# Dense v phase of a PEER layer: the gates of four experts per load in runs of 1 KB, in place of pairs in runs of 512 bytes

## The chip, the cores and the metric

One core of one Trainium2 chip runs the whole layer as one program. The metric is device time in microseconds, the median over runs. Everything is float32; most matmuls take operands that are split into a high and a low part (float32r), three matmuls for one product.

## What is computed

One layer of a streaming encoder over 1024 tokens of width 1024: gated mixing and attention, cross attention to a memory, then a PEER channel layer with 16384 single-neuron experts. Only the last part matters here:

```python
g = softmax(gv)                    # 128 picked experts per token
u = expert_u[idx_blk]
a = g_blk * gelu(einsum('tkd,td->tk', u, x_blk))
out = einsum('tk,tkd->td', a, expert_v[idx_blk])
h = layer_norm(DN_ALPHA * h + out)
```

## The kernel before

**Two ways for the experts.** The first 512 tokens (4 tiles, `GT`) fetch their picked rows of `expert_u` and `expert_v` by indirect DMAs that GpSimd issues (L1488), 128 rows of 4 KB each, into a ring of 8 slots (`ex_ring`). VectorE turns a u row tile into one dot per token (L1497); TensorE adds four v row tiles at a time into `ex_ps_v` (L1513, "values": 16 matmuls). The last 512 tokens (`DT` = 4 tiles) are computed densely over all 16384 experts, as 128 tiles of 128 experts. The dense u phase stores the activations of each expert tile to `act_d` in HBM (256 KB each). A gate phase then builds the gates of the 512 tokens and stores them to `gate_d`, whose shape is [8 token blocks, 128 partitions, 128 expert tiles, 64 tokens], so the 64 tokens of one expert tile are a run of 256 bytes and neighbouring expert tiles lie behind one another.

**The dense v phase** (from L1999 on) is the stage that the change touches. It multiplies activation by gate and adds a·v over the 128 expert tiles, in 32 groups of `GE` = 4. The gathers, dots and values of the first 512 tokens go on beside it. Its loop per expert tile e is:

- SyncE (queue q1, hardware_dynamic) loads a (`act_d`, 256 KB, L2045) once the low part of a of expert e-2 is done, and v (`expert_v`, 512 KB, L2050) once the low part of v of expert e-2 is done. The first four experts go through other buffers (L2038, L2039).
- SyncE loads gates for two expert tiles at a time with one DMA (`load_gates`, L2035): 128 partitions x 8 blocks, runs of 2 x 256 = 512 bytes, 512 KB. There are two buffers. After v of an even expert e it loads the pair e+2, e+3, once the product of expert e-1 is made, since that frees the buffer.
- ScalarE copies v to its high part (L2079), VectorE makes a times gate in place (`multiply`, L2108), ScalarE copies that to the high part of a (L2081), VectorE makes the low parts of v and a (L2113, L2115).
- VectorE then adds one finished PSUM tile of the group before to `eo_acc` (L2123; in the first group L2121), and does one dot of the gather tokens (L1497), the latter up to expert tile 67.

TensorE does a group when the low parts of its four experts are there: four token tiles, each of 24 matmuls of 128x512 (L110 to L112), with `values` between them. It writes two PSUM buffers in turn, so its tile t waits for VectorE's add of tile t-2. High and low parts have two group buffers. So VectorE works on group q+1 while TensorE works on group q, and each engine's order is written out by hand:

```python
for x in range(GE):
    multiply(q * GE + x)
    low_parts(q * GE + x)
    if q >= 1:
        add(q - 1, x)
    for _ in range(dots_b(q * GE + x)):
        dot(dve, done)
```

SyncE's queue is in order: a wait of one load holds back every load behind it. GpSimd's gathers run on queue q0 (software_dynamic), over the same 16 DMA engines.

Of the kernel before, what the change touches and what calls it, by code (L numbers as in the profile page):

```python
# [23 lines left out]
ALU = mybir.AluOpType  # L24
AX = mybir.AxisListType

P = 128
D = 1024
# [24 lines left out]
GBLK = 64  # L53
# [6 lines left out]
def layer_program(nc, x, mem, ln_in_g, ln_in_b, w_in, gate_ln_g, gate_ln_b, w_sp, b_sp, rel_bias, w_out,  # L60
# [4 lines left out]
    def dram(name, shape):  # L65
        return nc.dram_tensor(name, shape, F32, kind="Internal").ap()
# [15 lines left out]
    gate_d = dram("gate_d", [T // 2 // GBLK, P, P, GBLK])  # L82
# [3 lines left out]
    def sem(name):  # L86
        stage_sems.append(nc.alloc_semaphore(name=name))
        return stage_sems[-1]
# [7 lines left out]
    def local(stage):  # L96
        def sb(name, shape, dt=F32):
            return stage.enter_context(nc.sbuf_tensor(name, shape, dt))

        def pb(name, cols):  # L100
            return stage.enter_context(nc.psum_tensor(name, [P, cols], F32))
        return sb, pb
# [11 lines left out]
    with top:  # L114
# [16 lines left out]
        with ExitStack() as stage:  # L131
            sb, pb = local(stage)
# [1189 lines left out]
        def expert_stages(gain, bias, resid, dest):  # L1322
# [4 lines left out]
            DN = DT * P  # L1327
            ETILES = P
            RING, EXTRA, EXTRA_G = 8, 7, 5
            GE = 4  # L1330
            GROUPS = ETILES // GE
            NBLK = DN // GBLK
# [108 lines left out]
            gate_stored = [sem(f"ex_gate_stored{i}") for i in range(2)]  # L1441
            a_in = [sem(f"eo_a_in{i}") for i in range(2)]
            v_in = [sem(f"eo_v_in{i}") for i in range(2)]
            g_in = [sem(f"eo_g_in{i}") for i in range(2)]
            prod, a_hi_done, a_lo_done = sem("eo_prod"), sem("eo_a_hi"), sem("eo_a_lo")
            v_hi_done, v_lo_done = sem("eo_v_hi"), sem("eo_v_lo")
            out_mm = [sem(f"eo_mm{i}") for i in range(2)]
# [5 lines left out]
            with ExitStack() as whole:  # L1453
# [95 lines left out]
                with ExitStack() as gating:  # L1549
# [4 lines left out]
                    with ExitStack() as stage:  # L1554
                        sb, pb = local(stage)
# [328 lines left out]
                    with ExitStack() as stage:  # L1884
                        sb, pb = local(stage)
# [117 lines left out]
                with ExitStack() as stage:  # L2003
                    sb, pb = local(stage)
                    ln = RowNorm("eo_ln", sb, gain, bias, rows=(ring[:, 0, :], ring[:, 1, :]))
                    acc = sb("eo_acc", [P, DT, D])
                    a_sb, v_sb, g_raw = sb("eo_a_raw", [P, 2, DN]), sb("eo_v_raw", [P, 2, D]), sb("eo_g_raw", [P, 2, NBLK, 2, GBLK])
                    a_hi, a_lo = [w[:].rearrange("p (b x) t -> p b x t", b=2) for w in (late_hi, late_lo)]
                    v_hi, v_lo = sb("eo_v_hi_sb", [P, 2, GE, D], F32R), sb("eo_v_lo_sb", [P, 2, GE, D], F32R)
                    ps = [pb(f"eo_ps{i}", D) for i in range(2)]  # L2010
# [1 line left out]
                    def a_raw(e):  # L2012
                        return v_sb[:, e // 2, e % 2 * DN:(e % 2 + 1) * DN] if e < GE else a_sb[:, e % 2, :]

                    def v_raw(e):
                        return acc[:, e, :] if e < GE else v_sb[:, e % 2, :]

                    def loaded(eng, sems, e):
                        if e < GE:
                            eng.wait_ge(first_in[e], 32)  # L2020
                        else:
                            eng.wait_ge(sems[e % 2], 16 * ((e - GE) // 2 + 1))

                    def whole_row(j):
                        return xg[:, j, :] if j < GT else acc[:, j - GT, :]
# [3 lines left out]
                    with nc.Block() as block:  # L2029
                        @block.sync  # L2030
                        def _(sp):
                            def load_gates(r):
                                if r >= 2:
                                    sp.wait_ge(prod, 2 * (r - 1))
                                sp.dma_start(g_raw[:, r % 2, :, :, :], gate_d[:, :, 2 * r:2 * r + 2, :].rearrange("n p e t -> p n e t")).then_inc(g_in[r % 2], 16)  # L2035

                            for e in range(GE):
                                sp.dma_start(v_raw(e), v_rows[e, :, :]).then_inc(first_in[e], 16)  # L2038
                                sp.dma_start(a_raw(e), act_d[e, :, :]).then_inc(first_in[e], 16)  # L2039
                                if e % 2 == 0:  # L2040
                                    load_gates(e // 2)
                            for e in range(GE, ETILES):
                                if e >= GE + 2:
                                    sp.wait_ge(a_lo_done, e - 1)
                                sp.dma_start(a_raw(e), act_d[e, :, :]).then_inc(a_in[e % 2], 16)  # L2045
                                if e >= GE + 2:
                                    sp.wait_ge(v_lo_done, e - 1)
                                else:
                                    sp.wait_ge(a_lo_done, 2 * (e - GE + 1))
                                sp.dma_start(v_raw(e), v_rows[e, :, :]).then_inc(v_in[e % 2], 16)  # L2050
                                if e == GE:
                                    load_gates(GE // 2)
                                if e % 2 == 0 and e // 2 + 1 < ETILES // 2:
                                    load_gates(e // 2 + 1)
                                if e < 2 * GE:
                                    t = e - GE
                                    sp.wait_ge(v_lo_done, t + 1)
                                    sp.dma_start(acc[:, t, :], resid[(GT + t) * P:(GT + t + 1) * P, :]).then_inc(row_in[t], 16)
                                if e == LN_TILES * GE:
                                    sp.wait_ge(val_done, GT * P // 4)  # L2060
                                    ln.load(sp)
                            for j in range(TT):
                                sp.wait_ge(ln.ln_done, j + 1)
                                sp.dma_start(dest[j * P:(j + 1) * P, :], whole_row(j)).then_inc(stored, 16)
                            sp.wait_ge(stored, 16 * TT)
# [34 lines left out]
                        @block.vector  # L2100
                        def _(dve):
                            def multiply(e):
                                r = e // 2
                                loaded(dve, a_in, e)
                                if e % 2 == 0:
                                    dve.wait_ge(g_in[r % 2], 16 * (r // 2 + 1))
                                a = a_raw(e).rearrange("p (n t) -> p n t", t=GBLK)
                                dve.tensor_tensor(a, a, g_raw[:, r % 2, :, e % 2, :], ALU.mult).then_inc(prod, 1)  # L2108

                            def low_parts(e):  # L2110
                                b, x = e // GE % 2, e % GE
# [95 lines left out]
        free_sems()  # L2207
        early_stack.close()
        expert_stages(ln3_g, ln3_b, h2_d, out)
        act_stack.close()  # L2210

# [26 lines left out]
```

## Time and profile before

| What | Value |
|---|---|
| Median of 3 runs | 3495.75 us (3494.16 to 3499.4) |
| The profiled execution's own time | 3511.59 us |
| Its span | 3509.7 us |
| Mean granted TensorE clock | 0.94 |
| Dense v phase in it | first load 2582.7 us, first matmul 2611.3 us, last add about 3491 us |

The page divides the span into 40 slices of 87.7 us; the dense v phase is the last eleven. TensorE's row of the page is 9 (over 90% busy) in nearly all of them, and so is the DMA row until the last two. The time of the phase is therefore read from three things: how much TensorE idles in it, what VectorE, which feeds it, waits for, and what a load takes from its issue to its landing.

### The profile page before, as it was taken

Reading aid. Unit: us, or ns where it says so; the run is one execution under the profiler, and the core shown is the slowest. Engines: PE = TensorE matmul, PEld = TensorE weight load, DVE = VectorE, ACT = ScalarE, POOL = GpSimd, SP = SyncE. Lnnn points to the kernel's source line nnn. Section 1 sums busy time; section 2 is a strip of 40 time slices with the busy share of each in tenths; the row PEclk is TensorE's granted clock in tenths of the full one; section 3 lists DMA queues with packets and bytes.
Section 4 is the critical chain, followed back from the end, with each engine's and each line's share of the span. In section 5 each row is a group of like instructions: output and inputs, shape, how many; then the busy total and the mean of one; then the engine's idle time right before and its main releaser. Section 6 shows DMA issues by size and latency. Waiting matters only on the chain. (4 is left out here: it accounts for less than half of the span.)

```text
span 3509.7 us, 42739 instructions
## 1 busy us (share of the span) xinstructions
PE 3071.8 (88%) x16184; PEld 2393.6 (68%) x16184; DVE 2150.3 (61%) x4547; ACT 1137.3 (32%) x1739; POOL 1480.2 (42%) x1116
## 2 busy tenths in 40 slices
PE   3996888788879979999999999977749999999996
PEld 3875676677768867787777777655527676676665
DVE  4144684313545758987888776587737667654456
ACT  3212452312321114333333333287712222222222
POOL 3100102420120026885877677687734444434432
PEclk9997599899989989999999999988969999999998
DMA  4333003322222259999999999999999999989992
GB/s 159 102 108 119 20 2 126 125 88 65 107 102 63 71 207 351 412 408 374 408 410 402 410 410 383 374 365 406 410 348 344 357 378 383 373 304 372 374 350 100
DMA packets 367516, 936.06 MB, mean 267 GB/s; under 512 B 32832, under 2 KB 129736, under 8 KB 366288
## 3 DMA queue, kind: packets, MB, share of 16 engines
q0 software_dynamic: 147456, 536.94, 39.2%
q1 hardware_dynamic: 219856, 396.39, 31.4%
q8 instruction: 130, 2.13, 0.2%
q14 instruction: 74, 0.61, 0.0%
HBM read 825.53 MB, written 107.67 MB: 266 GB/s over the span
## 5 line engine op out<-in xcount | busy, mean ns | idle before, releaser
L1488 POOL DMA_INDIRECT ex_ring<-in_expert_v,ex_idxT_sb x405 | 475.8, 1175 | 513.8 <-PE ex_ps_v L1513 225.2
L1488 POOL DMA_INDIRECT ex_ring<-in_expert_u,ex_idx_sb x307 | 392.3, 1278 | 201.5 <-issue 87.8
L110 PE MATMUL eo_ps<-eo_v_hi_sb,aT_late_hi 128*128 128x512 f32 x1024 | 410.9, 401 | 41.5 <-DVE aT_late_lo L2115 41.5
L110 PE MATMUL ex_ps_h<-aT_late_hi,ex_uT_hi_sb 128*128 128x512 f32 x1024 | 415.4, 406 | 24.9 <-ACT ex_act L1656 12.4
L1497 DVE CUSTOM_DVE_ANT_0 ex_ring<-ex_ring,ex_xg 128x1024 f32<-128x1024 f32 x307 | 368.4, 1220 | 92.6 <-DMA ex_ring<-in_expert_u,ex_idx_sb 64.9
L112 PE MATMUL ex_ps_h<-aT_late_hi,ex_uT_lo_sb 128*128 128x512 f32 x1024 | 403.9, 394 | 0.0
L111 PE MATMUL eo_ps<-eo_v_lo_sb,aT_late_hi 128*128 128x512 f32 x1024 | 403.5, 394 | 0.0
L111 PE MATMUL ex_ps_h<-aT_late_lo,ex_uT_hi_sb 128*128 128x512 f32 x1024 | 402.7, 393 | 0.0
L112 PE MATMUL eo_ps<-eo_v_hi_sb,aT_late_lo 128*128 128x512 f32 x1024 | 402.3, 393 | 0.0
L2123 DVE TENSOR_TENSOR eo_acc<-eo_acc,eo_ps 128x1024 f32<-128x1024 f32 x124 | 151.4, 1221 | 280.8 <-PE eo_ps L112 215.2
L1513 PE MATMUL ex_ps_v<-ex_ring,ex_w_sb 128*32 128x512 f32 x1620 | 233.1, 629 | 75.6 <-DMA ex_ring<-in_expert_v,ex_idxT_sb 62.5
L1497 DVE CUSTOM_DVE_ANT_0 ex_ring_more<-ex_ring_more,ex_xg 128x1024 f32<-128x1024 f32 x193 | 230.5, 1220 | 100.9 <-DMA ex_ring_more<-in_expert_u,ex_idx_sb 74.6
L110 PEld LDWEIGHTS eo_ps<-eo_v_hi_sb,aT_late_hi 128*128 128x128 f32 x1024 | 194.6, 190 | 136.7 <-issue 52.8
L1488 POOL DMA_INDIRECT ex_ring_more<-in_expert_u,ex_idx_sb x193 | 246.1, 1275 | 70.6 <-issue 57.9
L110 PEld LDWEIGHTS ex_ps_h<-aT_late_hi,ex_uT_hi_sb 128*128 128x128 f32 x1024 | 194.4, 190 | 99.4 <-issue 51.3
L2079 ACT ACTIVATE eo_v_hi_sb<-eo_v_raw 128x1024 fp32r<-128x1024 f32 x124 | 131.3, 1059 | 395.6 <-DMA eo_v_raw<-in_expert_v 305.2
L1644 ACT ACTIVATE ex_uT_lo_sb<-ex_ps_t 128x1024 fp32r<-128x1024 f32 x128 | 131.7, 1029 | 373.6 <-PE ex_ps_t L1830 263.6
L112 PEld LDWEIGHTS ex_ps_h<-aT_late_hi,ex_uT_lo_sb 128*128 128x128 f32 x1024 | 194.7, 190 | 43.1
L112 PEld LDWEIGHTS eo_ps<-eo_v_hi_sb,aT_late_lo 128*128 128x128 f32 x1024 | 194.4, 190 | 42.3
L111 PEld LDWEIGHTS eo_ps<-eo_v_lo_sb,aT_late_hi 128*128 128x128 f32 x1024 | 194.6, 190 | 38.5
L111 PEld LDWEIGHTS ex_ps_h<-aT_late_lo,ex_uT_hi_sb 128*128 128x128 f32 x1024 | 195.0, 190 | 37.1
L2113 DVE TENSOR_TENSOR eo_v_lo_sb<-eo_v_raw,eo_v_hi_sb 128x1024 fp32r<-128x1024 f32 x124 | 157.9, 1274 | 32.6 <-ACT eo_v_hi_sb L2079 28.2
(351 smaller groups left out, 6445.4 us busy)
## 6 DMA issues: line engine op xcount, KB each, us to landing
ex_u_raw<-in_expert_u SPq DMA_DIRECT2D x128, 512.0 KB
eo_v_raw<-in_expert_v SPq DMA_DIRECT2D x124, 512.0 KB
act_d<-ex_act SPq DMA_DIRECT2D x128, 256.0 KB
gate_d<-ex_gate SPq DMA_DIRECT2D x8, 4096.0 KB, 15.1
eo_g_raw<-gate_d SPq DMA_DIRECT2D x64, 512.0 KB
eo_a_raw<-act_d SPq DMA_DIRECT2D x124, 256.0 KB
h_d<-n_row SPq DMA_DIRECT2D x24, 512.0 KB, 2.6
pin_raw<-in_w_in SPq DMA_DIRECT2D x20, 512.0 KB
```

Of the source, the lines that this page charges most:

```text
L110: pe.matmul(ps, l_hi, r_hi, start=first, stop=False)
L111: pe.matmul(ps, l_hi, r_lo, start=False, stop=False)
L112: return pe.matmul(ps, l_lo, r_hi, start=False, stop=last)
L1488: pool.indirect_dma_start(rows(n), None, table, bass.IndirectOffsetOnAxis(at, 0)).then_inc(ring_in[slot[n]], 16)
L1497: dve.tensor_tensor_reduce(out=u, in0=u, in1=xg[:, j, :], scale=1.0, scalar=0.0, op0=ALU.mult, op1=ALU.add, accum_out=hg[:, j, k:k + 1]).t ...
L1513: last = pe.matmul(ps_v[32 * q:32 * q + 32, col], spreads[:, q, 31 * i + 31:31 * i + 63], rows(at[q])[:, col], start=i == 0, stop=i == 31)
L1644: act.activation(uT_lo[:, e % 2, :, :], ps_t[e % 2][:].rearrange("p (k t) -> p k t", t=P), ACT.Copy).then_inc(uT_lo_done, 1)
L2079: act.activation(v_hi[:, b, x, :], v_raw(e), ACT.Copy).then_inc(v_hi_done, 1)
L2113: dve.tensor_tensor(v_lo[:, b, x, :], v_raw(e), v_hi[:, b, x, :], ALU.subtract).then_inc(v_lo_done, 1)
L2123: dve.tensor_tensor(acc[:, t, :], acc[:, t, :], ps[t % 2][:], ALU.add).then_inc(added[t % 2], 1)
```

## The change

Gates are loaded for a group of four expert tiles into one buffer of the same total size as the two before, [128, 8 blocks, 4 experts, 64 tokens]. The runs are 4 x 256 bytes = 1 KB. Each load is two DMAs of four blocks (512 KB each) on one semaphore, and the first product of the group waits for both (32). `load_gates(q)` comes after v of expert 4q, as a load did before, and with the same wait, that the product of expert 4q-1 is made. But what it loads is the gates of experts 4q to 4q+3, where it was those of 4q+2 and 4q+3. The load after v of expert 4q+2 is gone.

```diff
-            g_in = [sem(f"eo_g_in{i}") for i in range(2)]
+            g_in = sem("eo_g_in")
...
-g_raw = sb("eo_g_raw", [P, 2, NBLK, 2, GBLK])
+g_raw = sb("eo_g_raw", [P, NBLK, GE, GBLK])
...
-                            def load_gates(r):
-                                if r >= 2:
-                                    sp.wait_ge(prod, 2 * (r - 1))
-                                sp.dma_start(g_raw[:, r % 2, :, :, :], gate_d[:, :, 2 * r:2 * r + 2, :].rearrange("n p e t -> p n e t")).then_inc(g_in[r % 2], 16)
+                            def load_gates(q):
+                                if q >= 1:
+                                    sp.wait_ge(prod, GE * q)
+                                for h in range(2):
+                                    n = slice(h * NBLK // 2, (h + 1) * NBLK // 2)
+                                    sp.dma_start(g_raw[:, n, :, :], gate_d[n, :, GE * q:GE * (q + 1), :].rearrange("n p e t -> p n e t")).then_inc(g_in, 16)
...
-                                if e % 2 == 0:
-                                    load_gates(e // 2)
+                                if e == 0:
+                                    load_gates(0)
...
-                                if e == GE:
-                                    load_gates(GE // 2)
-                                if e % 2 == 0 and e // 2 + 1 < ETILES // 2:
-                                    load_gates(e // 2 + 1)
+                                if e % GE == 0:
+                                    load_gates(e // GE)
...
-                                r = e // 2
                                 loaded(dve, a_in, e)
-                                if e % 2 == 0:
-                                    dve.wait_ge(g_in[r % 2], 16 * (r // 2 + 1))
+                                if e % GE == 0:
+                                    dve.wait_ge(g_in, 32 * (e // GE + 1))
                                 a = a_raw(e).rearrange("p (n t) -> p n t", t=GBLK)
-                                dve.tensor_tensor(a, a, g_raw[:, r % 2, :, e % 2, :], ALU.mult).then_inc(prod, 1)
+                                dve.tensor_tensor(a, a, g_raw[:, :, e % GE, :], ALU.mult).then_inc(prod, 1)
```

## Rows read from the trace of the kernel before

**Rows 1.** Busy time by stage of the dense v phase (windows of the span).

```profile
core 0: us, PE busy (x) PEld busy (x) DVE busy (x) ACT busy (x) POOL busy (x), PEclk, DMA share, GB/s
2583.00:2611.00 28.00, 0.28 (x1) 0.00 (x0) 12.90 (x18) 7.42 (x9) 9.13 (x10) 0.50 1.01 363
2611.00:2700.00 89.00, 85.28 (x382) 63.99 (x383) 64.99 (x84) 22.81 (x28) 29.52 (x27) 0.94 0.93 339
2700.00:3100.00 400.00, 383.78 (x1870) 278.18 (x1870) 266.61 (x335) 98.27 (x119) 176.29 (x162) 1.00 1.00 368
3100.00:3400.00 300.00, 295.43 (x1503) 202.33 (x1502) 151.99 (x170) 70.75 (x86) 131.66 (x123) 1.00 0.98 359
3400.00:3491.00 91.00, 79.67 (x345) 62.00 (x344) 66.09 (x90) 25.10 (x33) 15.05 (x7) 0.94 0.41 144
```

**Rows 2.** Who waited for whom, 2700 to 3100 us: total, times, longest.

```profile
DVE eo_acc L2123 <- PE eo_ps L112: 82.2, 45, 4.6
DVE eo_acc L2123 <- issue: 25.2, 8, 4.8
PE ex_ps_v L1513 <- DMA ex_ring<-in_expert_v,ex_idxT_sb: 13.2, 13, 1.9
PE eo_ps L110 <- DVE aT_late_lo L2115: 3.1, 2, 2.6
```

**Rows 3.** Chain that ended last, pieces of 2738 to 3008 us: start, length, what.

```profile
2741.04 14.09 DMA eo_a_raw<-act_d
...
2857.01 1.22 DVE ex_ring L1497
...
2861.70 7.59 DMA ex_ring<-in_expert_v,ex_idxT_sb
...
2869.42 1.92 PE ex_ps_v L1513 x16
...
2882.16 9.32 DMA eo_v_raw<-in_expert_v
...
2894.81 8.37 DMA eo_v_raw<-in_expert_v
...
2906.15 12.49 DMA eo_a_raw<-act_d
...
2923.20 10.07 DMA eo_v_raw<-in_expert_v
...
2990.02 8.59 DMA eo_v_raw<-in_expert_v
```

**Rows 4.** DMA queues in 3432.4 to 3435.2 us: packets, MB, share of 16 engines.

```profile
DMA packets 1040, 0.52 MB, mean 187 GB/s; under 512 B 16, under 2 KB 1040, under 8 KB 1040
q1 hardware_dynamic: 1040, 0.52, 63.6%
```

**Rows 5.** DMA queues in 1532.3 to 1534.0 us (gathers beside one load of 1-KB runs).

```profile
q0 software_dynamic: 150, 0.55, 81.8%
q1 hardware_dynamic: 148, 0.13, 22.7%
```

**Rows 6.** DMA queues and gate issues in 2700 to 3100 us.

```profile
DMA packets 71535, 147.32 MB, mean 368 GB/s; under 512 B 4968, under 2 KB 35688, under 8 KB 71514
q0 software_dynamic: 23218, 84.54, 55.4%
eo_g_raw<-gate_d SPq DMA_DIRECT2D x29, 512.0 KB
```

**Rows 7.** VectorE in order of time, from expert 39's product to expert 43's.

```profile
2852.72 0.69 DVE L2108 TENSOR_TENSOR eo_a_raw<-eo_a_raw,eo_g_raw 128x512 f32<-128x512 f32 x1
...
2858.16 0.69 DVE L2108 TENSOR_TENSOR eo_a_raw<-eo_a_raw,eo_g_raw 128x512 f32<-128x512 f32 x1
...
2863.66 1.22 DVE L2123 TENSOR_TENSOR eo_acc<-eo_acc,eo_ps 128x1024 f32<-128x1024 f32 x1 [3.07 <-issue]
...
2865.94 0.69 DVE L2108 TENSOR_TENSOR eo_a_raw<-eo_a_raw,eo_g_raw 128x512 f32<-128x512 f32 x1
...
2869.09 1.22 DVE L2123 TENSOR_TENSOR eo_acc<-eo_acc,eo_ps 128x1024 f32<-128x1024 f32 x1 [0.69 <-PE eo_ps L112]
...
2877.06 1.22 DVE L2123 TENSOR_TENSOR eo_acc<-eo_acc,eo_ps 128x1024 f32<-128x1024 f32 x1 [3.24 <-PE eo_ps L112]
```

**Rows 8.** SyncE's queue: one gate load in the loaded stretch, one near the end.

```profile
2853.43 0.37 SPq L2035 DMA_DIRECT2D eo_g_raw<-gate_d  x1
...
3431.48 0.37 SPq L2035 DMA_DIRECT2D eo_g_raw<-gate_d  x1
```

**Rows 9.** VectorE in order of time at a later group boundary, without dots.

```profile
3226.51 0.69 DVE L2108 TENSOR_TENSOR eo_a_raw<-eo_a_raw,eo_g_raw 128x512 f32<-128x512 f32 x1
...
3233.97 1.22 DVE L2123 TENSOR_TENSOR eo_acc<-eo_acc,eo_ps 128x1024 f32<-128x1024 f32 x1 [5.04 <-issue]
3235.11 0.68 DVE L2108 TENSOR_TENSOR eo_a_raw<-eo_a_raw,eo_g_raw 128x512 f32<-128x512 f32 x1
```

**Rows 10.** VectorE in order of time, start of the phase.

```profile
2596.51 0.69 DVE L2108 TENSOR_TENSOR eo_v_raw<-eo_v_raw,eo_g_raw 128x512 f32<-128x512 f32 x1 [12.31 <-DMA eo_g_raw<-gate_d]
...
2600.86 0.69 DVE L2108 TENSOR_TENSOR eo_v_raw<-eo_v_raw,eo_g_raw 128x512 f32<-128x512 f32 x1 [1.93 <-DMA eo_v_raw<-act_d]
...
2605.38 0.69 DVE L2108 TENSOR_TENSOR eo_v_raw<-eo_v_raw,eo_g_raw 128x512 f32<-128x512 f32 x1 [0.46 <-DMA eo_g_raw<-gate_d]
...
2608.87 0.69 DVE L2108 TENSOR_TENSOR eo_v_raw<-eo_v_raw,eo_g_raw 128x512 f32<-128x512 f32 x1
...
2612.36 0.69 DVE L2108 TENSOR_TENSOR eo_a_raw<-eo_a_raw,eo_g_raw 128x512 f32<-128x512 f32 x1
...
2619.96 1.22 DVE L2121 SCALAR_TENSOR_TENSOR eo_acc<-eo_acc,eo_ps 128x1024 f32<-128x1024 f32 x1 [5.17 <-PE eo_ps L112]
```

**Rows 11.** The products by tile: count, durations and what they waited for.

```profile
L2108 DVE TENSOR_TENSOR eo_a_raw<-eo_a_raw,eo_g_raw x124: 680/686/721, 2612.4 to 3460.9; 128x512 f32<-128x512 f32 x124
L2035 SPq DMA_DIRECT2D eo_g_raw<-gate_d x64: 370/371/743, 2583.5 to 3431.5; - x64
  DMA eo_g_raw<-gate_d: 12.8, 2
```

**Rows 12.** The page's 40 slices of 87.7 us: GB/s that the DMA engines moved.

```profile
GB/s 159 102 108 119 20 2 126 125 88 65 107 102 63 71 207 351 412 408 374 408 410 402 410 410 383 374 365 406 410 348 344 357 378 383 373 304 372 374 350 100
```

More of the change, by code:

```diff
@@ L2006, in expert_stages @@
                     acc = sb("eo_acc", [P, DT, D])
-                    a_sb, v_sb, g_raw = sb("eo_a_raw", [P, 2, DN]), sb("eo_v_raw", [P, 2, D]), sb("eo_g_raw", [P, 2, NBLK, 2, GBLK])
+                    a_sb, v_sb, g_raw = sb("eo_a_raw", [P, 2, DN]), sb("eo_v_raw", [P, 2, D]), sb("eo_g_raw", [P, NBLK, GE, GBLK])
                     a_hi, a_lo = [w[:].rearrange("p (b x) t -> p b x t", b=2) for w in (late_hi, late_lo)]
```

## The prediction

> **What bounds the kernel now.** I read the busy time by stage first [rows 1]. From 2700 to 3400 us TensorE is busy 679 of 700 us, and the DMA share is 1.00 and 0.98. So this stage has two limits side by side: TensorE has 16.2 us of idle time in the first 400 us and 4.6 us in the next 300, and the DMA engines hardly rest. Then who waited for whom [rows 2]: VectorE's adds wait 107.4 us in 400 for TensorE's tiles, whereas TensorE waits only 3.1 us for low parts and 13.2 us for gathered v rows. VectorE, the one reader of the gates, therefore has slack: 29 gate loads of two experts in 400 us [rows 6] are 14.5 groups, one per 27.6 us, and 107.4 / 14.5 = 7.4 us of each group is waiting before adds. The chain that ended last [rows 3] passes through TensorE, and where it leaves it, it goes through transfers: gathers that a dot releases (7.6 us), v loads (8.4 to 10.1 us), and twice an a load that stands behind a gate load (14.1 and 12.5 us). The gates themselves stop a product only twice in the whole phase, 12.8 us together, both in the start [rows 10, 11].
>
> Two things can therefore move the time: a little less DMA work, and a gate load that now has to arrive within one step of VectorE, where it had three.
>
> **The sum, part by part.** It is made against the profiled execution of 3511.59 us (span 3509.7), and the difference is then put on the median of 3495.75, which is 15.8 us lower.
>
> 1. *Instructions.* 64 gate issues of 0.37 us become 32 x 2. SyncE's queue carries as many as before, GpSimd's queue isn't touched, the products read the same number of elements (686 ns) [rows 11]. At expert 4q the wait stands where it stood, with the same count; at 4q+2 it goes, but the next thing in the queue waits for a later event anyway (low part of a of 4q+1). Cost 0. The cover is that SyncE does nothing else.
>
> 2. *Packets.* A 512-byte packet costs 0.636 x 2.8 us x 16 / 1024 = 27.8 ns [rows 4] (1024 packets and 16 completion marks). A 1-KB packet costs 0.227 x 1.7 us x 16 / 128 = 48.2 ns [rows 5] (a 128-KB load of score rows, beside gathers). A 4-KB one costs 0.554 x 400 us x 16 / 20640 = 172 ns [rows 6] (84.54 MB are 20640 of them), 43 ns per KB. So 1 KB of gates goes from 55.6 to 48.2 ns, with bounds of 55.6 (no gain) and 43. There are 64 x 512 = 32768 KB: 15.2 us of 16 engines over the phase (0 to 25.8), 0.47 us per group. I take 48.2, as it is the same kind of load. How much arrives at the end? From 2611 to 3100 us (17.7 groups, 8.3 us saved) the chain goes through transfers part of the time; I give it half, -4 us, since TensorE's idle time there can give back no more than some 20 us in all (16.2 + 3.7). After 3100 TensorE is 98% busy [rows 1]: 0. Bounds: 0 and -16.
>
>    The Trainium skill (DMA: Bandwidth & Descriptors, Specifications) says that 512 bytes is the smallest transfer for line rate. By that rule the longer runs would bring nothing and this term would be 0; the rows at 27.8 and 48.2 ns speak against it, by 13% of the gates' share. The same page (Why small descriptors are slow) has a fixed cost of about 3 cycles per packet beside one per 32 bytes, so 38 cycles become 35, 8%; by that estimate the term would be -2.5 us.
>
> 3. *The exposed load.* Before, a load issued at the end of the product of 4q-1 was for experts 4q+2 on. Now it is for 4q, the very next product. In rows 7 the product of expert 39 ends at 2853.41, the gate load is issued at 2853.43 [rows 8], and the next product starts at 2858.16: 4.75 us. Without dots it is 7.9 us (3227.2 to 3235.1) [rows 9]. What does the load take? Idle, 1024 packets take 1.0 us to start and 2.6 us to move (issue at 3431.48, packets inside 3432.4 to 3435.2 [rows 4, 8]); 1024 packets of 1 KB 48.2 - 27.8 = 20.4 ns x 64 per engine = 1.3 us more, 5 us. Loaded, four v loads of the same queue take 9.1 us on average [rows 3]; they stand behind a gate load issued shortly before, so a gate load lands 1 to 2 us earlier than that, and the longer packets give 1.3 us back: 9 us. The bounds are 5 us and 14.1 us. So the first product of a group comes 9 - 4.75 = 4.2 us late while dots run.
>
>    Who is behind it on VectorE: low parts, the add of tile 0, a dot (which frees a gather slot), then the next expert. The waits before these adds are 3.07, 0.69 and 3.24 us [rows 7], so 4.2 us late becomes 1.2 at the first dot, 0.5 at the second, 0 at the third. TensorE needs the add of tile 0 only before tile 2, a whole tile (about 6.9 us) later, and the low parts only at the group's end: covered. What isn't covered is the gather behind a late dot, where it is on the chain. I take a quarter of a us per group of the 17 groups with dots: +4 us. Bounds: 0 (all covered), and the rival below. After expert 67 the boundary gap is 7.9 us, and the wait before the next add up to 5 us: 0. In the last two groups the DMA engines are nearly idle (0.41), the load takes 5 us: 0.
>
> 4. *What stands behind the gates on SyncE's queue.* a and v of expert 4q+1 now follow 1 MB, 1.3 us later than before, but their product starts later by more. a and v of 4q+3 have nothing before them any more and come up to 1.8 us earlier (1024 x 27.8 / 16). On the chain both kinds occur (the 14.1 and the 12.5 us are such a loads). 0, with -3 to +5.
>
> 5. *The start.* The first product waits 12.31 us for gates [rows 10]; that load is twice as large in as many packets, +1.3 us. The third product's 0.46 us wait for gates goes. First matmul +0.8 us, bounds -2 and +3. The gates of expert 4 are now issued after the product of expert 3 (2609.6) and land 6 to 7 us later, 4 us after the 2612.36 of before; the add behind them waits 5.17 us for TensorE [rows 10], so that is covered.
>
> Sum: 0 - 4 + 4 + 0 + 0.8 = +0.8 us, 3512.4 for the profiled execution, **3497 us** for the median, rounded up by half a us, as the bounds reach further up. About 0.2% (7 us) is what a measurement of this kernel can tell from no change.
>
> **The rivals.**
>
> *A. The DMA engines are the real limit of the dot stretch* (faster). For it: share 1.00 at 2700 to 3100, TensorE idle 16.2 us there, v loads and gathers on the chain. Then the whole saving of the stretch arrives, 8.3 us, and with shorter queues in front of gathers and of a and v of expert 4q+3 another 3: 3495.75 - 11 + 0.8 = 3485 us. Against it: TensorE's own work is 96% of the stretch, and 147.32 MB in 400 us is 368 GB/s, while the same engines moved 402 to 412 in most slices of the phase before [rows 12].
>
> *B. The single buffer closes a loop* (slower). Product of 4q-1, gate load, product of 4q, three more experts, next load. VectorE's step without waits is 7.78 - 3.07 = 4.71 us [rows 7], so the loop is 3 x 4.7 + 0.7 + L = 14.8 + L us. It decides above L = 27.6 - 14.8 = 12.8 us. Two of the transfers of rows 3 are above or near that, five are well below. If every load of groups 1 to 17 took 14.1 us, the period would be 28.9: +1.3 x 17 = 22 us, 3518. With half of them so, and late gathers besides, 3508.
>
> *C. The change doesn't do what it says* (slower): a 1-KB packet costs twice a 512-byte one beside the gathers, or the doubled burst delays the gathers released just then (the dot at 2857.0 and its gather at 2861.7 fall beside the load of 2853.43). Then term 2 is 0 and term 3 about doubles: +9, 3505 us.
>
> **How the numbers follow.** Forecast (all hidden or paid back, 3489 to 3502): 0.40. A 0.29, B 0.21, C 0.10. The range has to leave out 2 in 10: A's own bound is 3480, B's full price 3518, so 3480 to 3517. Faster by over 0.2% is A, 0.29; within it 0.40; slower B and C, 0.31. The likeliest case alone has 3489 to 3502.
>
> **What the profile of the changed kernel would show.** Queue q1 loses 32768 packets of 512 bytes at equal MB; if its share times the span doesn't fall by some 15 us, term 2 is wrong. The products of experts 4q wait for gates: some 3 us a time in the first 17 groups, 30 to 60 us in all, near none after expert 72. VectorE's waits for TensorE's tiles shrink by about as much. TensorE's idle time from 2700 to 3100 stays within some 8 us of 16.2. The first matmul comes at about 2612 us. I would be wrong if TensorE waits for low parts by tens of us (B), or if waits for gathers fall well below 13 us and the stretch shortens (A), or if the waits before products of experts 4q average over 6 us.

## The result and the profile after

**3543.3 us** median of 4 runs (3541.5 to 3556.9) against 3495.0 (4 runs) for the kernel before: ratio 1.0144, 95% interval 1.0117 to 1.0171, 48 us slower. The forecast was 3497, the range ended at 3517. The profiled execution took 3556.91 us (span 3555.0), 45.3 more than that of before. The dense v phase begins 6.0 us earlier in it, so the phase itself is some 51 us longer.

The windows of the dense v phase after the change, cut as in [rows 1] (its first load is at 2576.6 us, before at 2582.7):

```profile
core 0: us, PE busy (x) PEld busy (x) DVE busy (x) ACT busy (x) POOL busy (x), PEclk, DMA share, GB/s
2583.00:2611.00 28.00, 4.50 (x11) 3.58 (x12) 12.91 (x18) 6.53 (x8) 5.76 (x6) 0.50 0.94 345
2611.00:2700.00 89.00, 83.38 (x395) 63.21 (x394) 61.92 (x80) 21.91 (x27) 27.67 (x25) 1.00 0.89 327
2700.00:3100.00 400.00, 351.63 (x1647) 246.92 (x1645) 242.17 (x307) 87.66 (x105) 170.04 (x149) 0.94 0.91 332
3100.00:3400.00 300.00, 293.26 (x1477) 203.34 (x1474) 154.49 (x174) 71.92 (x88) 123.65 (x115) 0.99 0.94 350
3400.00:3536.00 136.00, 124.33 (x577) 91.70 (x576) 87.71 (x115) 35.37 (x45) 38.11 (x28) 0.96 0.62 221
```

The loss is in 2700 to 3100, where dots and gathers run: TensorE is idle 48.4 us there in place of 16.2, and does 1647 matmuls in place of 1870; the DMA share falls from 1.00 to 0.91. No engine is busier than before; they wait in turn. Who waited for whom, 2700 to 3100 (total, times, longest), against [rows 2]:

```profile
DVE eo_a_raw L2107 <- DMA eo_g_raw<-gate_d: 90.5, 13, 11.4
...
DVE eo_acc L2122 <- PE eo_ps L112: 58.1, 16, 8.7
...
PE ex_ps_v L1513 <- DMA ex_ring<-in_expert_v,ex_idxT_sb: 43.2, 13, 6.6
```

Each of the 13 groups stops VectorE at its first product for 7 us. VectorE's waits before its adds shrink from 107.4 us (82.2 for TensorE's tiles, 25.2 for nothing that the profile names) to 58.1, as the slack is eaten. And TensorE waits 43.2 us for gathered v rows, where it waited 13.2: that is 30 of the 32 us of new idle time. The groups of TensorE's lines in the same window, before the change and after it (busy, mean ns of one, idle before), say where the rest is:

```profile
L1513 PE MATMUL ex_ps_v<-ex_ring,ex_w_sb 128*32 128x512 f32 x448 | 53.9, 597 | 13.2 <-DMA ex_ring<-in_expert_v,ex_idxT_sb 13.2
```

```profile
L110 PE MATMUL eo_ps<-eo_v_hi_sb,aT_late_hi 128*128 128x512 f32 x416 | 166.9, 401 | 5.1 <-DVE eo_acc L2122 3.5 <-DVE aT_late_lo L2114 1.6
L111 PE MATMUL eo_ps<-eo_v_lo_sb,aT_late_hi 128*128 128x512 f32 x415 | 163.0, 393 | 0.0
L112 PE MATMUL eo_ps<-eo_v_hi_sb,aT_late_lo 128*128 128x512 f32 x416 | 162.7, 391 | 0.0
L1513 PE MATMUL ex_ps_v<-ex_ring,ex_w_sb 128*32 128x512 f32 x400 | 60.5, 731 | 43.3 <-DMA ex_ring<-in_expert_v,ex_idxT_sb 43.2
```

The dense matmuls run at their old speed. The values matmuls, which come right behind the wait, take 60.5 us for 400, where before's rate (53.9 / 448) gives 48.1: 12.4 us more. Windows of 5 us around one such wait show why:

```profile
2910.00:2915.00 5.00, 5.00 (x23) 4.13 (x22) 5.00 (x7) 1.70 (x2) 3.35 (x3) 1.00 0.73 257
2915.00:2920.00 5.00, 0.42 (x2) 0.00 (x0) 5.00 (x9) 0.63 (x1) 4.08 (x4) 0.81 0.93 304
2920.00:2925.00 5.00, 2.98 (x16) 0.67 (x16) 2.43 (x3) 1.58 (x2) 1.74 (x2) 0.51 1.00 395
2925.00:2930.00 5.00, 5.00 (x25) 3.90 (x22) 0.00 (x0) 0.00 (x0) 3.43 (x4) 1.00 1.04 389
```

TensorE stands still from 2915.4 to 2922.0, the granted clock falls to 0.51 (the lower level, 1.2 of 2.4 GHz), and most of the 16 values matmuls run at it. The chain has both cases: 16 values matmuls right behind a wait, and the next 16 with none before them.

```profile
2808.62 3.64 PE ex_ps_v L1513 x16
...
2823.39 1.85 PE ex_ps_v L1513 x16
```

Of the 25 sets of 16 in this window the eight behind the longest waits take 3.0 to 3.6 us and the other 17 some 1.9 each, and this difference is the whole 12.4 us. So a wait costs its own length and then slow matmuls: 30.0 + 12.4 us, and some 2 us before adds and low parts: 44 us in this window.

The chain that ended last shows the loop itself (start, length, what):

```profile
2859.99 0.37 SPq L2037
2860.40 15.66 DMA eo_g_raw<-gate_d
2876.15 0.69 DVE eo_a_raw L2107
2876.85 1.13 DVE eo_v_lo_sb L2112
2877.98 0.60 DVE aT_late_lo L2114
2878.58 1.13 DVE eo_acc L2122
2879.71 1.14 DVE ex_ring L1497
2880.86 0.60 DVE eo_a_raw L2107
...
2890.78 0.37 SPq L2037
2891.20 14.77 DMA eo_g_raw<-gate_d
2906.06 0.69 DVE eo_a_raw L2107
...
2921.05 17.42 DMA eo_g_raw<-gate_d
```

The load takes 15.66 us, then VectorE works with no wait from 2876.15 to 2890.77, from the product of expert 4q to that of 4q+3, then comes the next load: 30.8 and 29.9 us a round. The other gate loads on this chain are 16.86, 16.66 and 16.87 us. From TensorE's first matmul of group 1 to that of group 17 it is 30.2 us per group on average (27.2 before): 16 x 2.94 = 47 us. From group 17 to 31 it is 28.5 us (28.2 before), 4 us more over 14 of them.

### The profile page after: what moved, and what is told of

Its sections match the earlier page's. It is cut to its first block and busy times, and to the rows that moved or that the text cites. A ratio compares the mean times of both kernels' runs of the same rounds, so it can differ in the third digit from the quotient of the medians.

```text
span 3555.0 us, 42707 instructions
## 1 busy us (share of the span) xinstructions
PE 3086.1 (87%) x16184; PEld 2397.9 (67%) x16184; DVE 2150.1 (60%) x4547; ACT 1137.9 (32%) x1739; POOL 1487.2 (42%) x1116
## 3 DMA queue, kind: packets, MB, share of 16 engines
q1 hardware_dynamic: 187088, 396.39, 30.8%
## 5 line engine op out<-in xcount | busy, mean ns | idle before, releaser
L1488 POOL DMA_INDIRECT ex_ring<-in_expert_v,ex_idxT_sb x405 | 465.7, 1150 | 544.5 <-PE ex_ps_v L1513 253.3
L1513 PE MATMUL ex_ps_v<-ex_ring,ex_w_sb 128*32 128x512 f32 x1620 | 244.1, 658 | 114.6 <-DMA ex_ring<-in_expert_v,ex_idxT_sb 99.5
L1488 POOL DMA_INDIRECT ex_ring_more<-in_expert_u,ex_idx_sb x193 | 261.9, 1357 | 77.7 <-issue 57.0
L1513 PEld LDWEIGHTS ex_ps_v<-ex_ring,ex_w_sb 128*32 128x32 f32 x1620 | 52.3, 115 | 215.0 <-issue 213.5
```

What stands on the lines that cost most here:

```text
L1488: pool.indirect_dma_start(rows(n), None, table, bass.IndirectOffsetOnAxis(at, 0)).then_inc(ring_in[slot[n]], 16)
L1513: last = pe.matmul(ps_v[32 * q:32 * q + 32, col], spreads[:, q, 31 * i + 31:31 * i + 63], rows(at[q])[:, col], start=i == 0, stop=i == 31)
```

## The experiments

Ratios are to runs of the kernel before on the same chip, with 95% intervals. "Before" and "after" are the two kernels of this study.

**Is it the runs or the place of the load?** e1 keeps before's two buffers, counts and places and has the pair buffer filled in 1-KB runs (four experts, half of the blocks), so that some products take gates of another expert or block. e2 keeps 512-byte runs and loads both pairs where the changed kernel loads the four. e3 is the changed kernel with runs of 4 KB (16 experts of one block), again with other experts' gates.

```diff
 e1, against before
-  sp.dma_start(g_raw[:, r % 2, :, :, :], gate_d[:, :, 2 * r:2 * r + 2, :]...
+  half, quad = slice(r % 2 * NBLK // 2, (r % 2 + 1) * NBLK // 2), slice(r // 2 * GE, r // 2 * GE + GE)
+  sp.dma_start(g_raw[:, r % 2, :, :, :]..., gate_d[half, :, quad, :]...
 e2, against before
-      sp.wait_ge(prod, 2 * (r - 1))
+      sp.wait_ge(prod, r // 2 * GE)
-  if e % 2 == 0 and e // 2 + 1 < ETILES // 2:
+  if e % GE == 0:
+      load_gates(e // 2)
       load_gates(e // 2 + 1)
 e3, against after
-  n = slice(h * NBLK // 2, (h + 1) * NBLK // 2)
+  n, e0 = ..., 32 * (q % 4) + 16 * h
+  sp.dma_start(g_raw[:, n, :, :]..., gate_d[q // 4, :, e0:e0 + 16, :])
```

> The kernel before, its two pair buffers, places and waits untouched; only each 512-KB gate load reads 512 runs of 1 KB in place of 1024 runs of 512 bytes (it fetches half the blocks of a group of four experts, so products take gates of other experts and blocks). Theory (the late issue costs, not the runs): 16-engine time of gates falls by 15 us, the median is 3480 to 3495 us. Rival R (1-KB runs at this pitch are themselves dear or crowd the gathers): 3505 us or more.

> The kernel before with 512-byte runs and two pair buffers, but both pairs of a group are loaded where the changed kernel loads its four experts (after v of expert 4q, once the product of 4q-1 is made), and the first product of the group waits for both. Theory (late issue, and each packet may wait one turn behind a gather packet): 2048 packets in place of 1024, so the load takes longer than the 16.5 us of the changed kernel, 17 to 25 us, and the median is 3550 to 3640 us. Rival B (only the bytes of the burst count): as the changed kernel, 3543 within 7 us. Rival R (the runs are to blame): about 3500 us.

> The changed kernel with its timing and 2 x 512 KB per group, but each load reads 128 runs of 4 KB (gates of other experts), 256 packets per group in place of 1024. Theory (turns per packet): 16 packets per engine meet at most 16 gather packets of 172 ns, so the load takes 4 us of queue + about 6 us = 9 to 11 us, the loop 14.8 + 10 = 25 us is under TensorE's 27.6, and the median is 3490 to 3507 us. Rival B (bytes shared evenly between queues): the load still takes 14 to 17 us and the median stays within 10 us of 3543.

e1: 0.9983 (0.9950 to 1.0016). e2: 1.0217 (1.0147 to 1.0288). e3: 1.0025 (0.9994 to 1.0057). The times of e1, e2 and e3 came out as the first theory of each had it. Loading a whole group's gates late and together makes the loss, with 512-byte runs too; the 1-KB runs in the old places cost at most 0.2%. Whether the longer runs soften the loss isn't shown, since the intervals of e2 and of the changed kernel overlap. In e2 the same two waits of 2700 to 3100 are larger still:

```profile
DVE eo_a_raw L2109 <- DMA eo_g_raw<-gate_d: 107.3, 13, 16.0
...
PE ex_ps_v L1513 <- DMA ex_ring<-in_expert_v,ex_idxT_sb: 50.8, 13, 6.7
```

with gate loads of up to 20.2 us on its chain. In e3, with a fourth of the packets for the same bytes, two gate loads are on the chain of that window, and they are far shorter:

```profile
2870.88 10.66 DMA eo_g_raw<-gate_d
...
2955.57 10.57 DMA eo_g_raw<-gate_d
```

From the issue of a gate load to the start of the product that needs it, it is 9.4 us on average in this window (6.6 to 12.7), against 15.8 after the change. 14.6 + 10.6 = 25.2 us is under the 27.2 of a group before: a late load costs little (0.6% at most, perhaps nothing) if it is short enough.

**What makes the load long?** e9 loads pairs of 512-byte runs, each only when the product before it is made: twice as many exposed loads as after, each of as many packets (1024) but half the bytes. e10 and e11 are after and before with the ring's gathers cut to a quarter of each row (1 KB), so dots and values take the rest from what the slot held.

```diff
 e9, against before
-      sp.wait_ge(prod, 2 * (r - 1))
+      sp.wait_ge(prod, 2 * r)
-  if e % 2 == 0 and e // 2 + 1 < ETILES // 2:
-      load_gates(e // 2 + 1)
+  if e % 2 == 0:
+      load_gates(e // 2)
 e10, e11, against after and before
+  w = D if n < END_G else D // 4
-  pool.indirect_dma_start(rows(n), None, table, ...
+  pool.indirect_dma_start(rows(n)[:, 0:w], None, table.rearrange("r (a c) -> (r a) c", c=w), ...
```

> The kernel before with 512-byte runs and pairs, but each pair is loaded only once the product just before the pair is made (one product ahead in place of three), so 512 KB are exposed twice per group. Theory: a load of 1024 packets takes 11 to 16 us beside the gathers as in the changed kernel, whatever its bytes, so a pair's loop is 4.7 + 0.7 + L = 16 to 21 us, 33 to 42 us per group in the dot stretch: 60 to 150 us slower than before, worse than the changed kernel. Rival (bytes count): half the bytes land in half the time, 8 us, the loop is 2 x 13.5 = 27 us, and it is within 15 us of before.

> The changed kernel; in the dense v phase each gather fetches 1 KB per row in place of 4 KB (other bytes, so dots and values of that phase are of other data). All instructions and waits stay. Theory (the gate load is long because gather packets stand between its own): the load takes 6 to 9 us instead of 16, the loop of 15 + 8 = 23 us is under TensorE's time, and the kernel is within 8 us of the next control. Rival (the load's length is its own, from its packets and their pitch in HBM): it takes 13 us or more and the distance to the control stays 35 us or more.

> Control: the kernel before with the same short gathers. Both theories: 5 to 25 us faster than before, since values and dots no longer wait for gathers.

e9: 1.0127 (1.0103 to 1.0151), 40 us. Both expectations missed the time (60 us or more, 15 at most); on the length of a load the rival, that bytes count, was right with its 8 us. The waits are many (197.5 us at 50 products) but the loads short. The chain has seven of 7.9 to 8.3 us in a row, three of them:

```profile
2795.69 7.93 DMA eo_g_raw<-gate_d
2807.91 8.04 DMA eo_g_raw<-gate_d
2821.38 7.90 DMA eo_g_raw<-gate_d
```

e10: 0.9909 (0.9893 to 0.9926), e11: 0.9904 (0.9886 to 0.9922). With short gathers, the changed kernel and the kernel before differ by 3 us (3461.8 and 3458.6), as the theory had it. Against the kernel before with whole gathers e11 is 36 us faster, more than the 5 to 25 that were expected. The windows 2700 to 3100 of e10 and of e11:

```profile
2700.00:3100.00 400.00, 400.00 (x1954) 291.67 (x1952) 275.82 (x343) 102.16 (x125) 175.23 (x162) 1.00 0.65 217
```

```profile
2700.00:3100.00 400.00, 400.00 (x1960) 290.38 (x1959) 277.50 (x345) 104.58 (x127) 175.08 (x160) 1.00 0.67 217
```

TensorE never rests in either. The place and the bytes of the load are the same as after, so the gathers beside it make its length. The table is from the packets in the traces: for the gate loads issued between 2690 and 3080 us, the mean time from issue to last packet, and what the gather queue moved between first and last packet (e8, e12 and e15 are described below):

| kernel | load, packets of | us | gathers beside it, MB | their GB/s |
|---|---|---|---|---|
| before | 1024 of 512 B | 8.2 | 1.10 | 185 |
| e1, early, longer runs | 512 of 1 KB | 6.7 | 0.69 | 149 |
| e9, late pairs | 1024 of 512 B | 7.6 | 0.81 | 156 |
| after | 1024 of 1 KB | 15.1 | 2.74 | 244 |
| e2, late pairs together | 2048 of 512 B | 16.7 | 3.04 | 239 |
| e12, one group ahead | 1024 of 1 KB | 10.4 | 1.50 | 170 |
| e15, as e12 | 1024 of 1 KB | 10.3 | 1.39 | 169 |
| e8, after, 6 ring slots | 1024 of 1 KB | 8.1 | 0.85 | 125 |
| e10, after, short gathers | 1024 of 1 KB | 5.2 | 0.10 | 25 |

A load that lasts longer meets more gathers by that alone, so the megabytes don't prove the cause; e10 does, and the last column, a rate, doesn't have this fault. Two things make the 15 us together. The load has twice the bytes: half of them in the late place take 7.6 us (e9), no longer than before. And it stands in a dense stretch of gathers: the same bytes one group ahead take 10.4 us (e12).

Why the gathers are dense just there is argued from the order of the rows, no run tests it by itself. While VectorE waits it frees no slot, and then dots come 4.65 us apart (rows 2879.71, 2884.37 and 2889.01 of the chain, and a fourth behind the next load's issue), each with a new 512-KB gather, and values free four more slots; the next gate load is issued right behind them. At its issue 1.01 MB of gathers are issued and not yet moved, against 0.84 before and 0.38 in e12. If that is the reason, the loop feeds itself.

**Does it help to take the dots out of the loop?** e4 makes all dots of a group before its first product.

```diff
+  for _ in range(sum(dots_b(q * GE + x) for x in range(GE))):
+      dot(dve, done)
+      done += 1
   for x in range(GE):
...
-      for _ in range(dots_b(q * GE + x)):
-          dot(dve, done)
-          done += 1
```

> The changed kernel with VectorE's order changed: all dots of a group come before its first product, so they run while the gates are under way. Theory (a loop of product, load, three more experts, load bounds the dot stretch; late dots make gathers late): three dots of 1.2 us leave the loop, 14.8 + 16.5 = 31.3 becomes 27.7 us, and no dot waits for gates: 3500 to 3515 us. Rival (TensorE loses to the DMA burst itself, that is to gathers slowed by it): 3535 us or more.

e4: 1.0241 (1.0184 to 1.0298), a miss for the theory; the rival's time came true, but by another path. The gate loads did get short (8.6 us beside 0.70 MB), but other waits of 2700 to 3100 took their place:

```profile
DVE ex_ring L1497 <- DMA ex_ring<-in_expert_u,ex_idx_sb: 99.8, 17, 11.6
...
PE eo_ps L110 <- DVE eo_acc L2122: 53.7, 12, 8.7
```

Four dots in a row outrun their gathers, VectorE waits for those, and its adds come too late for TensorE.

**A second buffer of four.** There is no room for one beside the ring. e6 takes ring slots 6 and 7; e7 and e8 are before and after with a ring of 6, as controls.

```diff
 e6, e7, e8
-  slot.append((n - END_G) % RING)
+  slot.append((n - END_G) % (RING - 2))
 e6 besides, against after
+  g_raw = [sb("eo_g_raw", ...), ring[:, 6:8, :]...]
-  if q >= 1:
-      sp.wait_ge(prod, GE * q)
+  if q >= 2:
+      sp.wait_ge(prod, GE * (q - 1))
+  if e % GE == 0 and e // GE + 1 < GROUPS:
+      load_gates(e // GE + 1)
```

> The changed kernel's loads (2 x 512 KB of 1-KB runs per group) with a second buffer, so that each group's gates are loaded one group ahead, once the last product of the group before last is made. The buffer lies in two slots of the gather ring, which has 6 slots in the dense v phase; so it is to be read against the kernel before with 6 slots. Theory (exposure alone costs): it equals that control or is up to 12 us faster, and no product waits for gates after the first. Rival (the burst of 1 MB hurts gathers, a and v by itself): 15 us or more above that control.

> Control: the kernel before with 6 ring slots in the dense v phase. Both theories: 0 to 30 us slower than before, since two gathers fewer are under way.

> Control: the changed kernel with 6 ring slots in the dense v phase. Theory: at most 6 gathers, in place of 8, can stand beside the gate load, so the load lands 1 to 4 us sooner, and the time is 25 to 50 us above the control of the kernel before with 6 slots. Rival (gathers do not set the load's time): the load takes the same 15 to 17 us and the distance stays 48 us or more.

e6: 1.0415 (1.0376 to 1.0454), e7: 1.0437 (1.0384 to 1.0491), e8: 1.0428 (1.0374 to 1.0482). Two slots fewer cost 145 us (3653.7 against 3508.4) where 30 at most were expected, and hide everything else: all three are equal, and nothing follows for the buffer. e8 misses both of its expectations (25 us or more above e7; it is 5). Its late loads took only 8.1 us, beside gathers at half the rate of after: with fewer gathers under way, the late load is short and the change costs nothing that can be measured.

**The second buffer elsewhere.** e12 parks two tiles of `ex_xg` (1 MB, unused until the layer norm) in HBM, puts the second buffer there and loads each group of four one group ahead. e13 is the control: before, with the same tiles parked and used as ring slots 8 and 9.

```diff
 e12, against after
+  g_raw = [sb("eo_g_raw", ...), xg[:, 0:2, :]...]
+  sp.wait_ge(sum_g, 2)
+  sp.dma_start(park_d..., xg[:, 0:2, :]).then_inc(parked, 16)
-  if e % GE == 0:
-      load_gates(e // GE)
+  if e % GE == 0 and e // GE + 1 < GROUPS - 1:
+      load_gates(e // GE + 1)
   if e == LN_TILES * GE:
+      sp.dma_start(xg[:, 0:2, :], park_d...).then_inc(back, 16)
 e13, against before (parking as in e12)
-  slot.append((n - END_G) % RING)
+  slot.append((n - END_G) % (RING + 2))
```

> The changed kernel's loads (2 x 512 KB of 1-KB runs per group) with a second buffer and the full ring of 8 slots. The buffer is the place of the first two finished token tiles, which are written to HBM (1 MB) at the start of the phase and read back before their norm; gates are loaded one group ahead from group 1 to 30. Theory (the missing lead of the load is the whole loss): all of the 48 us come back, the median is 3485 to 3500 us on the scale of 3495, and no product between expert 8 and 123 waits for gates. Rival (bursts of 1 MB or 1-KB runs cost by themselves): 3515 us or more.

> The kernel before with the same two tiles parked in HBM, the place used for two more slots of the gather ring (10 in place of 8) in the dense v phase; gates as before. Since 6 slots cost 150 us, gathers have little to spare at 8. If TensorE's waits for gathers are the rest of the loss in the dot stretch, 10 slots give 5 to 20 us: 3475 to 3490 us. If more gathers under way only lengthen the a, v and gate loads, 3495 us or more.

e12: 1.0075 (1.0046 to 1.0103), 3522 us on the scale of 3495, which is the rival's side. e13: 0.9987 (0.9956 to 1.0018), 3491 us: ten slots with the parking equal eight without it, less than the theory's gain. So the lead gives about half of the 48 us back. Its products no longer wait for gates, but v loads of up to 17 us stand on its chain: SyncE issues them behind two gate loads, 1 MB in one piece. That alone proves nothing, since e13's chain has v loads of 17.4 and 18.7 us at no loss of time. e14 issues the second half two experts later; e15 is e12 again, on e14's chip.

```diff
 e14, against e12
-  if e % GE == 0 and e // GE + 1 < GROUPS - 1:
-      load_gates(e // GE + 1)
+  if e % (GE // 2) == 0 and e // GE + 1 < GROUPS - 1:
+      load_gates(e // GE + 1, (e % GE // 2,))
```

> e12 (a second buffer for four experts' gates, each load one group ahead, runs of 1 KB) with the two 512-KB halves of a load issued two experts apart, after v of expert 4q and after v of expert 4q+2, in place of one behind the other. Theory (what is left of e12's excess is the 1-MB burst ahead of SyncE's next loads of a and v): the loads of v on the chain of waits, 9.7 to 17.1 us in e12, come back to 8 to 11 us as before the change; the time is within 0.4% of the kernel before on the same chip (ratio 0.996 to 1.004). Rival (the rest lies elsewhere: the lead shares the gathers' bandwidth in a worse place whatever the size of the piece, or the first execution's chip was at fault): the ratio stays at 1.005 or above, and the chain's loads of v stay above 11 us.

> e12 once more, on the same chip as e14, since e12's one comparison was made on a chip whose runs of the kernel before lay 20 us apart. Both theories: 1.005 to 1.010 again, and by theory above e14. If it comes within 0.4% of the kernel before, e12's excess was that chip's, and the lead alone gives the whole loss back.

e14: 1.0022 (1.0008 to 1.0036). e15: 1.0052 (1.0034 to 1.0071). ScalarE's wait for v in 2700 to 3100, in e15 and then in e14:

```profile
ACT eo_v_hi_sb L2096 <- DMA eo_v_raw<-in_expert_v: 177.9, 46, 15.1
```

```profile
ACT eo_v_hi_sb L2096 <- DMA eo_v_raw<-in_expert_v: 126.0, 47, 5.9
```

The longest wait for v falls from 15.1 to 5.9 us, e15's chain has a v load of 19.05 us in this window and e14's has none, and TensorE waits 12.6 us for gathers in e14 (23.1 in e15, 13.2 before). Both came out as their theories had it, though the intervals of e14 and e15 just touch. A lead with the load in two pieces brings the time back to within 0.2% (8 us on that chip) of the kernel before; e14 parks its tiles as e12 does, so the parking costs no more than that.

**The 1-KB runs with the old places and the right gates.** e5 changes the layout in HBM, so that two blocks of 64 tokens lie side by side: a pair of experts is then in runs of 1 KB, and the gate phase stores runs of 256 bytes.

```diff
-  gate_d = dram("gate_d", [T // 2 // GBLK, P, P, GBLK])
+  gate_d = dram("gate_d", [T // 4 // GBLK, P, P, 2 * GBLK])
-  sp.dma_start(gate_d[n], gate_sb[:, n % 2, :, :])
+  sp.dma_start(gate_d[n // 2, :, :, n % 2 * GBLK:(n % 2 + 1) * GBLK], gate_sb[:, n % 2, :, :])
```

> The kernel before, all its waits and places kept, with another layout of the gates in HBM: two token blocks side by side, so that the same pair loads read runs of 1 KB with the right gates; the gate phase then stores runs of 256 bytes in place of whole contiguous blocks. Theory: -5 us in the dense v phase as in the run of the runs alone, +0 to +20 us in the gate phase for 8 stores of 4 MB in 16384 packets each; 3490 to 3510 us on the scale of 3495. Rival (stores of short runs are hidden behind that phase's other work): 3490 us or below.

e5: 1.0114 (1.0073 to 1.0154), 3536 us on that scale, a miss for both. The dense v phase isn't slower than before (TensorE 382.65 us busy in 2700 to 3100; from first load to last product 863 us, before 879, e1 870, one execution each), but it begins 65 us later, since the stores made the gate phase longer. The store's row of the page's DMA issues, before the change and in e5 (KB each, median us to landing):

```profile
gate_d<-ex_gate SPq DMA_DIRECT2D x8, 4096.0 KB, 15.1
```

```profile
gate_d<-ex_gate SPq DMA_DIRECT2D x8, 4096.0 KB, 56.3
```

And ScalarE's wait for them in e5 (total, times, longest), which the kernel before doesn't have at this size:

```profile
ACT ex_gate L1932 <- DMA gate_d<-ex_gate: 82.7, 4, 27.6
```

No variant that does all the work beats the kernel before by more than its measurement is uncertain.

## Why the prediction was wrong

The step that failed is part 3, "The exposed load", by its term L: "9 us" with a top bound of 14.1. On the chain it was 14.8 to 17.4 us, and 15.1 on average by the packets (9.9 to 17.2). The rest of that step follows from this size: not 3 us of waiting per product of experts 4q but 7 in 2700 to 3100 (160.6 us at 28 products in all), and not +4 us but some +50. The text's own sign of being wrong, waits of over 6 us on average, came true. Against "near none after expert 72", ten products from expert 80 on waited 45 us together, but TensorE hardly felt it (293.3 of 300 us busy from 3100 to 3400).

*How L was mis-sized.* It was read from v loads of 512 KB (the gate loads of before took 8.2 us), and the second 512 KB of the new load were priced at 1.3 us, from packets with nothing beside them. One group ahead the 1 MB took 10.4 us (e12), 2.2 more than the 512 KB of before; in the late place 15.1, which adds 4.7. I took a transfer's length as a property of the transfer. It depends on what else the engines have to move, and there the change put it beside gathers at 244 GB/s in place of 185. The top bound of 14.1, which was one load of `act_d`, lies below the new mean.

*Rival B was the mechanism.* Its loop, "three more experts" and 14.8 + L, is right to 0.2 us (14.6 measured). Its threshold of 12.8 us for L is only bracketed: 9.4 us cost little (e3), 15 cost 1.4%. Its price was built on L of 14.1 for all groups (+22 us) and a group of 27.6 us; the measured rounds of 30.2 against 27.2 us make 47. Two things differ from its text. Its sign was to be "TensorE waits for low parts by tens of us"; that wait was 1.6 us. The late dots reach TensorE through the ring: dot, slot, gather, values. And nothing in it had the granted clock, 12.4 of the 44 us in the window.

*Packets (part 2).* q1 has 32768 packets fewer at equal MB, as said. Its rows of the whole page, before, after and in e1 (packets, MB, share of 16 engines):

```profile
q1 hardware_dynamic: 219856, 396.39, 31.4%
```

```profile
q1 hardware_dynamic: 187088, 396.39, 30.8%
```

```profile
q1 hardware_dynamic: 187088, 396.39, 31.1%
```

Its share times the span is 1095 us in place of 1102 (30.8% of 3555.0, 31.4% of 3509.7), and 1087 in e1: 7 and 15 us less, where 15.2 were worked out, with some 2 us of rounding in each. By the text's sign ("some 15 us") term 2 holds in e1 and not in the changed kernel. The gate packets themselves cost what was worked out: from 2700 to 3100 us a 512-byte one took 29.0 ns before, a 1-KB one 48.2 after (49.8 in e1). The saving is real but small, and e1's 0.9983, whose interval takes in 1, leaves -4 us standing and excludes more than 17. The Trainium skill (DMA: Bandwidth & Descriptors, Specifications) has line rate from 512 bytes on; by that rule the packets would bring nothing. The traces speak against it for the packets, 58.0 (two of 29.0) against 48.2 ns per KB; on the kernel's time no run here tells the two apart.

*Rival A* (the saving arrives in full, 11 us) isn't excluded by e1. In the changed kernel it had no chance: over the 400 us the DMA share fell to 0.91, so the engines weren't the limit (they are full in stretches, as from 2920 to 2930 us at 1.00 and 1.04). *Rival C*'s first half is excluded by the 48.2 ns, and 1-KB runs in the old place cost the kernel 6 us at most (e1). Its second half, gathers delayed by the doubled burst, wasn't tried by itself.

*Instructions, queue, start (parts 1, 4, 5).* The first matmul comes 29.9 us after the first load of the phase (2576.6 to 2606.5); before it was 28.7 (2582.6 to 2611.3). That is +1.2 us, against the "+0.8" of the text. Part 1's cost of nothing on SyncE stands. Part 4 can't be told apart in the changed kernel; e15 and e14 show that its kind of cost is real when the gates come as 1 MB in one piece ahead of a and v: 12 us (3509.6 to 3497.8), with intervals that just touch. It was priced at -3 to +5.

*What bounds the kernel.* Of the 107.4 us that the text puts down to TensorE's tiles, 25.2 have no releaser in the profile [rows 2]. The group of 27.6 us is 400 us over the loads in it; by TensorE's first matmuls it was 27.2.

## What to carry to other kernels

Before a load is moved behind the event that needs it, write down the loop that it closes and ask what else that event releases: a load's length in the old trace, beside other traffic, is no bound for its length in the new place, and its second half is not priced from idle engines. If the loop comes within a few us of the bounding engine's period, count the late engine's other duties (here the dots that free ring slots) as part of it, and TensorE's slower matmuls behind a wait. Keep the lead before the packet size: 512-byte packets with a lead beat 1-KB packets without one by 48 us, and where the lead needs a large load, it is issued in pieces between the loads that are due.

## What the runs showed of the hardware

- Eight stores of 4 MB in runs of 256 bytes take 56.3 us from issue to landing (median), in place of 15.1 in contiguous blocks (e5, before).
- A gate packet of 512 bytes took 29.0 ns of its DMA engine, one of 1 KB 48.2 (before and after, 2700 to 3100 us).
- A load of 1 MB in 1-KB runs took 15.1 us beside gathers at 244 GB/s, 10.4 at 170 and 5.2 at 25 (after, e12, e10).
- Behind a wait TensorE's granted clock stood at 0.51 while the next matmuls ran (window 2920 to 2925); over 400 us the matmuls behind waits took 12.4 us longer, beside 30.0 us more of waiting.
- The gather ring has a sharp knee: against 8 slots, 6 cost 4.4% (e7) and 10 bring nothing (e13).
